# Hybrid attention and MoE encoder step on one core: scores, P transposes and V products regrouped, two heads side by side

## What is computed

```
m = silu(c) @ w_ada + b_ada -> shift1, scale1, gate1, shift2, scale2, gate2
h = RMSNorm(x) * (1 + scale1) + shift1
q, k, v, B, C, u, g_attn, g_conv = split(h @ w_in)
q, k = RMSNorm per head of 64            # 16 heads of q, 4 of k and v
s = q @ k.T * 64**-0.5 + bias            # chunks of 64; a chunk reads itself and the two before
p = exp(s - m);  den = sum(p) + exp(sink - m);  m = max(max(s), sink)
A = (p / den) @ v
conv = conv_w[0]*u_all[t] + conv_w[1]*u_all[t+1] + conv_w[2]*u_all[t+2],  u_all = [state, C*u]
x = x + gate1 * ((sigmoid(g_attn)*A + sigmoid(g_conv)*B*conv) @ w_out)
x = x + gate2 * HierMoE(RMSNorm(x)*(1+scale2)+shift2)   # top 1 of 8 groups, top 2 of 8 experts
```

## Time and profile before

| What | Value |
|---|---|
| Median of 3 runs | 1710.36 us (1706.1 to 1715.13) |
| The profiled execution, its own time | 1714.0 us |
| Its span in the trace | 1712.5 us |
| Mean granted TensorE clock | 0.903 of full speed |
| PE / PEld busy | 1408.8 us (82%) / 839.9 us (49%) |
| DVE / ACT / POOL busy | 469.0 us (27%) / 240.9 us (14%) / 371.5 us (22%) |
| The loop over `j`, eight iterations | 109.96 to 615.68 us |

### The profile page before, as it was taken

How to read it: one execution, slowest core, us unless ns; L and a number is a source line. 1 busy time by engine, 2 the same in 40 slices (tenths; PEclk the granted TensorE clock), 3 DMA queues, 4 the chain that set the end, 5 groups by cost and what they waited for, 6 DMA issues and landing times.

```text
span 1712.5 us, 22191 instructions
## 1 busy us (share of the span) xinstructions
PE 1408.8 (82%) x7954; PEld 839.9 (49%) x7955; DVE 469.0 (27%) x998; ACT 240.9 (14%) x500; POOL 371.5 (22%) x582
## 2 busy tenths in 40 slices
PE   3579998999999999389898988888787777778883
PEld 2578897897897865233333333333233332323331
DVE  1524415415414425512122211112111121111214
ACT  2313223222222311101010100000000000000000
POOL 2443433433432100111111111111111111111111
PEclk9687989889887999699999999889999999998997
DMA  9432313312322172499999699999999999999984
GB/s 332 147 95 97 111 50 104 113 53 91 116 71 70 33 268 98 165 417 423 426 405 423 261 426 426 425 427 425 425 421 422 423 422 423 406 420 411 414 336 172
DMA packets 112162, 479.24 MB, mean 280 GB/s; under 512 B 15452, under 2 KB 67836, under 8 KB 87788
## 3 DMA queue, kind: packets, MB, share of 16 engines
q1 hardware_dynamic: 95312, 457.85, 66.3%
q0 software_dynamic: 13248, 13.59, 2.7%
q10 hardware_dynamic: 3580, 7.51, 1.3%
HBM read 483.18 MB, written 24.46 MB: 296 GB/s over the span
## 4 chain that ended last, share of the span: by engine, by line
PE 50%; DMA 35%; DVE 6%; ACT 4%; issue 4%; SPq 1%; ACTq 0%; POOL 0%; DVEq 0%; POOLq 0%
DMA ws<-in_w_up 24%; PE ps L953 18%; PE ps L736 14%; DMA ws<-in_w_gate 6%; PE ps L965 4%; PE ps L798 3%; PE ps L867 3%; PE ps L829 3%; ACT arena L1109 2%; DVE arena L1289 2%; DMA ws<-in_w_in 2%; DMA ws<-in_w_down 1%; PE ps L816 1%; PE ps L699 1%; DVE small L1312 1%
## 5 line engine op out<-in xcount | busy, mean ns | idle before, releaser
L953 PE MATMUL ps<-ws,arena 128*64 128x512 f32 x1920 | 469.7, 647 | 121.2 <-DMA ws<-in_w_gate 76.1
L953 PEld LDWEIGHTS ps<-ws,arena 128*64 128x64 f32 x1920 | 165.1, 148 | 424.3 <-issue 424.3
L736 PE MATMUL ps<-ws_r 128*128 128x274 f32 x1600 | 299.2, 307 | 9.7 <-issue 9.7
L385 POOL TENSOR_TENSOR held<-small 128x1 f32<-128x1 f32 x225 | 44.7, 198 | 987.5 <-DMA yc_dram<-arena,cur 291.4
L736 PEld LDWEIGHTS ps<-ws_r 128*128 128x128 f32 x1600 | 249.1, 203 | 16.4 <-issue 14.9
L965 PE MATMUL ps<-ws,arena 128*64 128x512 f32 x960 | 212.6, 595 | 32.8 <-DMA ws<-in_w_down 25.2
L1517 DVE TENSOR_TENSOR misc<-misc,ps 128x512 f32<-128x512 f32 x33 | 22.7, 688 | 596.0 <-PE ps L953 596.0
L736 PE MATMUL ps<-arena_r,ws_r 128*128 128x274 f32 x800 | 175.3, 302 | 0.0
L965 PEld LDWEIGHTS ps<-ws,arena 128*64 128x64 f32 x960 | 75.4, 137 | 149.3 <-issue 111.4
L736 PEld LDWEIGHTS ps<-arena_r,ws_r 128*128 128x128 f32 x800 | 136.2, 203 | 0.0
L568 POOL TENSOR_TENSOR ws_r<-ws,ws_r 128x1024 fp32r<-128x1024 f32 x48 | 117.2, 2442 | 3.8
(11 more groups left out here) (273 smaller groups left out, 1236.6 us busy)
## 6 DMA issues: line engine op xcount, KB each, us to landing
ws<-in_w_gate SPq DMA_DIRECT2D x59, 2048.0 KB, 16.2
ws<-in_w_up SPq DMA_DIRECT2D x59, 2048.0 KB
ws<-in_w_down SPq DMA_DIRECT2D x59, 2048.0 KB, 19.3
ws<-in_w_ada SPq DMA_DIRECT2D x12, 2048.0 KB, 8.9
ws<-in_w_in SPq DMA_DIRECT2D x48, 512.0 KB, 3.8
merged<-in_w_gate SPq DMA_DIRECT2D x3, 2048.0 KB, 17.6
arena<-in_w_up SPq DMA_DIRECT2D x3, 2048.0 KB, 15.8
arena<-in_w_down SPq DMA_DIRECT2D x3, 2048.0 KB, 14.8
```

The lines of the kernel that those rows point to most:

```text
L385: return eng.tensor_tensor(cell, epsc, epsc, ALU.add)
L736: last = nc.tensor.matmul(ps[:, 2 * buf + h, 0:HALF], w[:, k, :], x[:, k, HALF * h:HALF * h + HALF], start=(k == 0 and part == 0), stop=(k ...
L953: last = nc.tensor.matmul(ps[CAP * e:CAP * e + CAP, m, :], xT[c][:, k, CAP * e:CAP * e + CAP], weights[e][:, k, :], start=(k == 0), stop=( ...
```

## The change

The scores of the two heads of a tile are now issued one right behind the other, into four PSUM banks instead of two (`S_BANK`). K of head 0 lies in partitions 0 to 63, that of head 1 in 64 to 127. `ITEMS` now runs over tiles outside and heads inside. VectorE computes the negated scores and their minimum, with the negated sink as the start value, so the ten small operations on maxima are gone; ScalarE takes each exponential as soon as its item is there, and undoes the sign by `scale=-1.0`. VectorE divides P by the denominators before it is transposed (ten operations at the new L1319) instead of dividing the output. The V product has its operands exchanged: V (64 columns) is the stationary operand and transposed P moves, and the two heads' results land in partitions 0 to 63 and 64 to 127 of one bank, already transposed. So `osb`, its division and the five output transposes go. All P transposes and V products now stand behind step 4 instead of behind step 3 (`PV_AT` holds 7 everywhere: behind the last part of the projection), with one ScalarE copy of up to 512 columns a tile. `sumsq` moves into step 1, behind its second of eight parts, `ada` from ahead of step 1 to behind it, and ScalarE's root ahead of its copy of C.

```
+        S_BANK = ((4, 6), (5, 7))
+        PT_BANK = (4, 5)
+        O_BANK, OS_BANK = 7, 6
+        ITEMS = [(t, hh) for t in range(NTT) for hh in range(2)]
...
+                def scores(t):
+                    if t == 0:
+                        pe.wait_ge(qn_rdy, j + 1)
+                        pe.wait_ge(kcur_rdy, 2 * j + 2)
+                        pe.wait_ge(ss_used, 3 + j)
+                    if t == 1:
+                        pe.wait_ge(ada_evac, j + 1)
+                    if t >= 2:
+                        pe.wait_ge(ttr_done, 10 * j + (2 * t - 2))
+                    for hh in range(2):
+                        nc.tensor.matmul(ps[:, S_BANK[t % 2][hh], 0:n], qT[HD * hh:HD * hh + HD, c0:c0 + P],
+                                         kcur[HD * hh:HD * hh + HD, k0:k0 + n], start=True, stop=True).then_inc(s_mm, 1)
+                def p_transposes(t):
+                    pe.wait_ge(pn_rdy, 5 * j + (t + 1))
+                    if t >= 2:
+                        pe.wait_ge(pT_rdy, 5 * j + (t - 1))
+                    for kk in range(w0 // P, 2):
+                        for hh in range(2):
+                            last = nc.tensor.transpose(ps[0:m, PT_BANK[t % 2], at:at + P],
+                                                       s_all[:, 2 * t + hh, P * kk:P * kk + m], ident[:, :])
+                def p_times_v(t):
+                    pe.wait_ge(pT_rdy, 5 * j + (t + 1))
+                    for kk in range(first, 2):
+                        for hh in range(2):
+                            r = slice(HD * hh, HD * hh + HD)
+                            dst = ps[r, O_BANK, P * t:P * t + P] if t < 4 else ps[r, OS_BANK, 0:DEC]
+                            last = nc.tensor.matmul(dst, vcur[0:m, tile, :], pT[0:m, t % 2, kk, hh, 0:rows],
+                                                    start=(kk == first), stop=(kk == 1))
+                step(0, 0, a_free, 1 + 3 * j)
+                step(1, 1, b_free, 1 + 3 * j, [(1, q_sumsq)])
+                ada(None, 0, 5, 0, 16 * j + 32)
+                step(2, 0, a_free, 2 + 3 * j, [(k, scores, t) for t, k in enumerate(S_AT)])
+                step(3, 1, b_free, 2 + 3 * j)
+                step(4, 0, a_free, 3 + 3 * j, [(k, p_transposes if what == "T" else p_times_v, t) for k, what, t in PV_AT])
                 step(5, 1, b_free, 3 + 3 * j)
...
+                    act.wait_ge(ttr_done, 10 * j + (i + 1))
                     nc.scalar.activation(s_all[0:rows, i, w0:w0 + n], s_all[0:rows, i, w0:w0 + n], ACT.Exp,
-                                         bias=negm[0:rows, i:i + 1], accum_out=den[0:rows, i:i + 1])
+                                         bias=negm[0:rows, i:i + 1], scale=-1.0, accum_out=den[0:rows, i:i + 1])
...
+                dve.wait_ge(exp_rdy, j + 1)
+                ch(V.tensor_tensor(den, den, es, ALU.add))
+                ch(V.reciprocal(den, den))
+                for i, (t, hh) in enumerate(ITEMS):
+                    last = V.tensor_scalar(s_all[0:rows, i, w0:w0 + n], s_all[0:rows, i, w0:w0 + n], den[0:rows, i:i + 1],
+                                           None, ALU.mult)
+                    if hh == 1:
+                        last.then_inc(pn_rdy, 1)
...
-                pool.wait_ge(pv_mm, 10 * j + 10)
+                pool.wait_ge(pv_mm, 5 * j + 5)
```

More of the change, by code:

```diff
@@ L385, in hold @@
             return eng.tensor_tensor(cell, epsc, epsc, ALU.add)
-        S_BANK, PT_BANK = (4, 6), (5, 4)
-        ITEMS = [(hh, t) for hh in range(2) for t in range(NTT)]
+        S_BANK = ((4, 6), (5, 7))
+        PT_BANK = (4, 5)
+        O_BANK, OS_BANK = 7, 6
+        S_AT = (7, 7, 7, 7, 7)
+        PV_AT = tuple((7, what, t) for what, t in (("T", 0), ("T", 1), ("V", 0), ("T", 2), ("V", 1), ("T", 3), ("V", 2), ("T", 4),
+                                                   ("V", 3), ("V", 4)))
+        ITEMS = [(t, hh) for t in range(NTT) for hh in range(2)]
         def window(t):
@@ L738, in project @@
                                                     start=(k == 0 and part == 0), stop=(k == KT8 - 1 and part == 2))
-                last.then_inc(proj_mm, 1)
+                    if k == KT8 - 1:
+                        last.then_inc(proj_mm, 1)
+                    for at, what, *arg in hooks:
+                        if at == k:
+                            what(*arg)
             def sumsq():
@@ L789, in _ @@
-                sumsq()
-                step(2, 0, a_free, 2 + 3 * j)
-                pe.wait_ge(qn_rdy, j + 1)
-                pe.wait_ge(kcur_rdy, 2 * j + 2)
-                for i, (hh, t) in enumerate(ITEMS):
-                    c0, rows, _ = TILES[t]
-                    k0, w0, n = window(t)
-                    if i >= 2:
-                        pe.wait_ge(ttr_done, 10 * j + (i - 1))
-                    nc.tensor.matmul(ps[:, S_BANK[i % 2], 0:n],
-                                     qT[HD * hh:HD * hh + HD, c0:c0 + P],
-                                     kcur[HD * hh:HD * hh + HD, k0:k0 + n],
-                                     start=True, stop=True).then_inc(s_mm, 1)
@@ L808, in p_transposes @@
+                def p_times_v(t):
                     rows = TILES[t][1]
                     _, w0, n = window(t)
-                    if i == 0:
-                        pe.wait_ge(exp_rdy, j + 1)
-                    if i >= 2:
-                        pe.wait_ge(pT_rdy, 10 * j + (i - 1))
-                    for kk in range(w0 // P, 2):
-                        m = min(P, n - P * kk + w0)
-                        last = nc.tensor.transpose(ps[0:m, PT_BANK[i % 2], P * kk:P * kk + P],
-                                                   s_all[:, i, P * kk:P * kk + m], ident[:, :])
@@ L828, in p_times_v @@
                         tile = (t - 1 + kk) if t < 4 else 4 + kk
-                        last = nc.tensor.matmul(ps[0:rows, 6 + hh, HD * t:HD * t + HD],
-                                                pT[0:m, i % 2, P * kk:P * kk + rows],
-                                                vcur[0:m, tile, :],
-                                                start=(kk == first), stop=(kk == 1))
-                    last.then_inc(pv_mm, 1)
-                p_transposes(0)
-                for i in range(10):
-                    if i < 9:
-                        p_transposes(i + 1)
-                    p_times_v(i)
-                step(4, 0, a_free, 3 + 3 * j)
-                pe.wait_ge(o_rdy, j + 1)
-                for t, (_, rows, _) in enumerate(TILES):
-                    dst = ps[:, 4, P * t:P * t + P] if t < 4 else ps[:, 5, 0:DEC]
-                    last = nc.tensor.transpose(dst, osb[0:rows, t, :], ident[0:rows, 0:rows])
-                last.then_inc(oT_mm, 1)
+                        for hh in range(2):
[3 more added lines that the diff above has]
+                                                    start=(kk == first), stop=(kk == 1))
+                    last.then_inc(pv_mm, 1)
+                step(0, 0, a_free, 1 + 3 * j)
[4 more added lines that the diff above has]
+                step(4, 0, a_free, 3 + 3 * j, [(k, p_transposes if what == "T" else p_times_v, t) for k, what, t in PV_AT])
                 step(5, 1, b_free, 3 + 3 * j)
@@ L1109, in _ @@
                     nc.scalar.activation(s_all[0:rows, i, w0:w0 + n], s_all[0:rows, i, w0:w0 + n], ACT.Exp,
-                                         bias=negm[0:rows, i:i + 1], accum_out=den[0:rows, i:i + 1])
-                nc.scalar.activation(es, es, ACT.Exp).then_inc(exp_rdy, 1)
+                                         bias=negm[0:rows, i:i + 1], scale=-1.0, accum_out=den[0:rows, i:i + 1])
+                for hh in range(2):
+                    last = nc.scalar.activation(es[:, hh:10:2], negm[:, hh:10:2], ACT.Exp, bias=skp[:, hh:hh + 1])
@@ L1277, in _ @@
             dve.wait_ge(kout_st, 32)
-            for i in (4, 9):
+            for i in (8, 9):
                 V.memset(s_all[:, i, :], 0.0)
```

116 lines of the change are left out of this document (48 added, 68 removed).

## The result

The changed kernel takes 1600.39 us (median of 4 runs, 1597.34 to 1603.11), the kernel before in the same comparison 1712.42. The ratio is 0.935, 95% interval 0.9317 to 0.9383. The profiled execution took 1597.34 us with a span of 1595.9, against 1714.0 and 1712.5. That is 117 us less; forecast were 94, in a range that holds the result.

What follows compares the result with a forecast made beforehand. Bound taken: TensorE's work and waits in the loop over `j`, for which everything behind waits. 40.2 + 4.4 + 5.8 = 50.4 us, eight times 403; with start and clock loss 94 us less than 1714.0: 1620, or 1616 against the median; range 1594 to 1655.

Steps and rivals of the forecast that it cites:

- Projections, ada and sumsq: Per iteration on TensorE: six projections 37.3 us, ada 2.05, sums of squares 0.82 with no wait; sum 40.2.
- The wait for q: TensorE's 1.42 us wait ahead of the scores for q to be scaled goes to zero in each iteration.
- Scores: Score block per iteration: 0.52 to first item, 3.1 for six items, 0.7 behind; 4.4 us, bounds 4.1 and 6.7.
- P block: Transposes and V products per iteration: 3.9 us for three tiles, 0.9 filling, 1.0 short tiles; 5.8, bounds 4.4 and 8.2.
- P's division: VectorE's ten pieces about 2.8 us, slowed beside POOL; done about 12 us after scores began, 4 to 5 us of cover.
- The clock: Granted clock in the loop: half of the iterations lose 1.7 us, half of a 3.4 us stretch; 7 us in all.
- The sum: Loop of eight iterations at 50.4 us, 403, plus 1.8 at the start and 7 for clock loss: 94 us less.
- D: Rival: array shape changes make the kernel slower; at 1.3 us more each, 30 us lost, 1745 us; chance 0.03.
- A: Rival: clock still falls in scores and P block of every iteration, +47 us, 1663 us; chance 0.15.
- B: Rival: heads side by side do not overlap, V products double, 12 us in all, 1628 us; chance 0.08.
- C: Rival: TensorE waits for P's division because VectorE stands behind POOL, 3 us an iteration, +24, 1640 us; chance 0.08.
- E: Rival: the change moves stalls and takes none, loop the same 505 us, 1712 us; chance 0.02.

Runs made afterwards that it cites:

- scores_by_head: Changed kernel with its ten score matmuls ordered all tiles of head 0, then all of head 1, in the same four banks: 1603.31 us, ratio 0.9362.
- old_q_early: Kernel before with only q's chain moved early (sums of squares inside second projection, ada behind it, root ahead of copy of C): 1704.94 us, ratio 0.9957.
- old_both: Kernel before with q's chain early and P block behind the fifth projection, still one head at a time, P undivided: 1651.63 us, ratio 0.9659.
- the probes: Changed kernel with four extra small matmuls in each sixth projection, stationary operand 128 wide or 64 wide: 1610.17 and 1615.27 us.
- t_spread: Changed kernel with P transposes issued between parts of the fifth projection, each transposed P written over its P: 1594.34 us, ratio 0.9298.

## Why the prediction was right, and where it was not

- **What bounds.** Right: what the loop saved (111 us) came off the end whole; the profiled executions differ by 117.
- **Projections, ada and sumsq.** 40.2 forecast; the chain's rows above (13.96, 0.06, 1.19, 4.57, 1.89, 6.32, 12.43) sum to 40.4. No wait at the new place of `sumsq`, 0.06 us of issue, but the sums of squares take 1.19 us in the chain where 0.82 was forecast; ada takes 0.16 less than forecast.
- **The wait for q.** Gone, as forecast.
- **Scores.** 4.4 forecast, 3.67 measured. The mis-sized term is six items at VectorE's pace, 3.1 us: the chain has 2.7 (328.42 to 331.10), with 0.45 for 0.52 ahead of them and 0.54 for 0.7 behind. The pace of an item, 0.57 us (0.55 in the earlier trace rows), was read between starts in the old kernel. In the timeline of the changed one the items of 256 columns start 0.46 to 0.47 us apart, although the operation itself is longer (0.48 against 0.415 us). Through that stretch the old chain goes by TensorE's score matmuls and not by VectorE, and in scores_by_head the old order has the short starts too, with four banks. So the old starts were not VectorE's own pace but what two banks allow.

```profile
329.09 0.15 DVE L384 COPY held<-small 128x1 f32<-128x1 f32 x1
329.16 0.48 DVE L1306 CUSTOM_DVE_ANT_0 arena<-ps,arena,small 128x256 f32<-128x256 f32 x1
...
329.56 0.16 DVE L384 COPY held<-small 128x1 f32<-128x1 f32 x1
```

The old chain there:

```profile
391.26 1.26 PE ps L798 x4
```

- **P block.** 5.8 forecast, 5.02 measured, in the lower half between the bounds of 4.4 and 8.2. Both terms were a little large: a round is 1.17 us (0.58 and 0.59) for 1.3, and filling 0.7 for 0.9.
- **P's division.** The place and the mechanism were right: 5.88 us for ten pieces, which take 2.47 in the iteration without POOL (2.8 forecast); done 12.4 us after the first score, forecast 12, with 3.7 us of cover, forecast 4 to 5. The run with the block one projection earlier showed the cover gone and the wait there, 0.89 us.
- **The clock.** This is the step that failed. I took 7 us of loss; there was none. The term was half of the iterations with a stretch of 3.4 us; no row of the kernel before shows such a stretch, its shortest fall inside the loop lasts 6.8 us. The reason I gave, that both falls follow a wait that goes, holds for the P block alone. With two banks and no wait (old_q_early, old_both) the clock still fell at the scores in 8 and 7 of 8 iterations. With four banks and no wait it did not fall once, whether heads were side by side or not. With four banks and the wait it fell twice in eight, with two banks and the wait, all else the same but the order of the heads, in all eight. So the falls in the scores came from the slow two-bank scores first, with the wait as an addition. Not run was the changed kernel with early q and two banks; the two-bank kernels without the wait differ from it in the P block as well. That the forecast of the clock came out near all the same was luck: four banks, which I had not counted as what keeps the clock up, were part of the change.
- **The sum.** Score block 0.7, P block 0.8 and clock 0.9 an iteration less than forecast and the projections 0.2 more are 2.2, times eight 17 to 18 us: the 17 by which the loop's saving of 111 us exceeds the 94 forecast. The sizes were on the cautious side. Two slips of adding change nothing: 1616 - 21 is 1595 (1596 stands there), and D at 30 us lost is 1740 to 1744 (1745 stands there).
- **Rivals.** A did not happen. B, priced at 12 us, did not happen either, but what it is about is cheap: side by side is worth 0.17 us an iteration in the scores and 0.46 in the P block, 5 us of 112, as far as the two orders tested tell. C stands 3.7 us away. D: a change of shape costs 0.10 us net, at most about 0.16; 1.2 each would have turned the sign. The Trainium skill (TensorEngine Tiling (Array Packing), Key Properties) says that a change of mode drains TensorE; the probes agree that there is a cost and put it at 0.10 us net. E did not happen.

Of the change's own title, then, "two heads side by side" is the small part. What carried it: the P block's place, which with q early took 56 us off the old kernel (1651.63), and the rest, four banks, exchanged operands and divided P, which took 51 more and brought the clock to 1.00. How these 51 divide is not measured directly; in the changed kernel with late q the two banks more are worth 34 us (1647.47 against 1613.30).

## What to carry to other kernels

Price a wait together with the clock behind it: the wait for q removed alone gave 0.4% here, where its 1.42 us an iteration are 0.7%, because falls of the clock at the next wait took part of it back; the P block moved alone gave 2.5%, both together 3.4%. Give a producer of PSUM results that another engine must read more banks before giving it more parallelism; four banks did in the scores what pairing was meant for. And before work on VectorE that reads and writes SBUF only is put ahead of TensorE, lay POOL's timeline beside it and count how long both run.

## What the runs showed of the hardware that I had not expected

- A change between a 128-wide and a 64-wide stationary operand cost 0.10 us of TensorE net (0.82 us for eight, between two kernels that differ in the width alone, and with it in the time of the probes' weight loads); the idle rows of weight loads had suggested 0.15 to 0.20.
- A P block of transposes and products in turn, 5 us long, ran at a granted clock of 1.00 in all eight iterations of the changed kernel; transposes in this mixture did not bring the clock down. The Trainium skill (TensorE: Matmul & The Clock Gate, Part 4) says that full clock does not engage for them; by the rows here they at least did not end it.
- VectorE's pass over two SBUF operands (L1334) took 2.77 us beside POOL's subtraction and 0.73 without, and ten passes over one operand (L1319) took 5.88 and 2.47, so it is not only single-operand work that waits.
- With V as the moving operand a row of the timeline has 1.11 us for eight instructions, and the chain has 0.97 for the same eight, 0.121 each; with V as the stationary one thirty-six took 2.00 us of the chain in t_spread, 0.056 each. What of this is the exchange of operands and what the order no run tells apart.
